# Six block-product groups per column pair, and sums of the features laid out anew, in the last matrix product of a two-block transformer kernel

## The reference, cut to what matters

```python
def conv_ffn(h, w_up, conv_w, conv_b, w_down):
    S = h.shape[1]
    val, gate = jnp.split(h @ w_up, 2, axis=-1)
    gp = jnp.pad(gate, ((0, 0), (CONV_W - 1, 0), (0, 0)))
    g = conv_b
    for i in range(CONV_W):
        g = g + conv_w[i] * gp[:, i:i + S]
    return (jax.nn.silu(g) * val) @ w_down
    ...
        x = x + conv_ffn(rms_norm_2(x, norm_ffn[l]), w_up[l], conv_w[l], conv_b[l], w_down[l])
    return rms_norm_2(x, norm_final)
```

## Time and profile before

| | |
|---|---|
| median of 3 runs | 2433.54 us (2433.43 to 2433.71) |
| the profiled execution: its own time | 2433.6 us |
| its span | 2431.8 us |
| TensorE, busy | 2421.5 us |
| VectorE, busy | 1717.2 us |
| ScalarE, busy | 1381.1 us |
| GpSimd, busy | 83.4 us |

### The profile page before, as it was taken

The page is one execution under the profiler, slowest core; times in us unless marked ns, Lnnn a source line. Parts: engine busy times, 40 slices in busy tenths (PEclk is TensorE's granted clock), DMA queues, the critical chain, the costliest instruction groups (busy, mean ns, idle before and its releaser), DMA issues.

```text
span 2431.8 us, 34028 instructions
## 1 busy us (share of the span) xinstructions
PE 2421.5 (100%) x12669; PEld 2081.3 (86%) x12669; DVE 1717.2 (71%) x2079; ACT 1381.1 (57%) x1830; POOL 83.4 (3%) x101
## 2 busy tenths in 40 slices
PE   9999999999999999999999999999999999999998
PEld 8888888888889999888888888888988888888877
DVE  7675757888765656786656767665666666679997
ACT  6444444556656666565755556565645545556655
POOL 0000000001100000010000000000000000000001
PEclk9999999999999999999999999999999999999999
DMA  8666666676556554575585564455566665657775
GB/s 314 199 189 185 188 188 184 197 243 216 182 175 181 178 160 144 210 230 191 163 237 165 157 176 146 165 180 156 174 188 181 186 193 179 188 173 211 240 233 162
DMA packets 237363, 462.46 MB, mean 190 GB/s; under 512 B 15265, under 2 KB 60753, under 8 KB 236220
## 3 DMA queue, kind: packets, MB, share of 16 engines
q1 hardware_dynamic: 230960, 435.94, 57.5%
q0 software_dynamic: 5888, 24.34, 3.8%
q10 hardware_dynamic: 396, 0.59, 0.2%
HBM read 448.68 MB, written 2.69 MB: 186 GB/s over the span
## 4 chain that ended last, share of the span: by engine, by line
PE 98%; DVE 1%; ACT 0%; DMA 0%; issue 0%; ACTq 0%; SPq 0%; DVEq 0%
PE ps L835 25%; PE ps L837 13%; PE ps L801 12%; PE ps L803 12%; PE ps L802 12%; PE ps L985 6%; PE ps L986 6%; PE ps L987 6%; PE ps L759 1%; PE ps L868 1%; PE ps L866 1%; PE ps L867 1%; PE ps L1473 1%; PE ps L1244 0%; PE ps L1232 0%; PE ps L1431 0%
## 5 line engine op out<-in xcount | busy, mean ns | idle before, releaser
L2468 DVE TENSOR_TENSOR w_lo<-raw,w_hi 128x1024 fp32r<-128x1024 f32 x689 | 842.3, 1228 | 465.5 <-ACT w_hi L1643 444.8
L1643 ACT ACTIVATE w_hi<-raw 128x1024 fp32r<-128x1024 f32 x689 | 727.0, 1060 | 650.6 <-PE ps L837 358.0
L835 PE MATMUL ps<-x_hi_lo,w_hi 128*128 128x512 f32 x2336 | 820.9, 394 | 1.1 <-DVE w_lo L2643 1.1
L837 PE MATMUL ps<-x_hi_lo,w_lo 128*128 128x256 f32 x2336 | 660.7, 283 | 0.0
L835 PEld LDWEIGHTS ps<-x_hi_lo,w_hi 128*128 128x128 f32 x2336 | 438.7, 188 | 102.7 <-issue 1.2
L801 PE MATMUL ps<-w_hi,x_hi_lo 128*128 128x512 f32 (+3 forms) x1184 | 461.9, 390 | 0.0
L803 PE MATMUL ps<-w_hi,x_hi_lo 128*128 128x512 f32 (+3 forms) x1184 | 453.8, 383 | 0.0
L802 PE MATMUL ps<-w_lo,x_hi_lo 128*128 128x512 f32 (+3 forms) x1184 | 452.6, 382 | 0.0
L837 PEld LDWEIGHTS ps<-x_hi_lo,w_lo 128*128 128x128 f32 x2336 | 439.2, 188 | 0.0
L1820 ACT ACTIVATE w_hi<-raw 128x1024 fp32r<-128x1024 f32 x207 | 215.5, 1051 | 159.8 <-PE ps L987 135.5
L2476 DVE TENSOR_TENSOR w_lo<-raw,w_hi 128x1024 fp32r<-128x1024 f32 x207 | 248.8, 1222 | 34.4 <-ACT w_hi L1820 34.0
(11 more groups left out here) (469 smaller groups left out, 2732.3 us busy)
## 6 DMA issues: line engine op xcount, KB each, us to landing
raw<-in_w_up SPq DMA_DIRECT2D x160, 512.0 KB, 3.8
raw<-in_pool_w_in SPq DMA_DIRECT2D x126, 512.0 KB, 4.0
raw<-in_w_in SPq DMA_DIRECT2D x96, 480.0 KB, 3.9
raw<-in_w_down SPq DMA_DIRECT2D x84, 512.0 KB, 5.3
raw<-in_pool_w_out SPq DMA_DIRECT2D x64, 512.0 KB, 5.3
raw<-in_ple_w_gate SPq DMA_DIRECT2D x64, 512.0 KB, 4.3
raw<-in_mla_w_in SPq DMA_DIRECT2D x56, 448.0 KB, 3.6
raw<-in_pool_w_group SPq DMA_DIRECT2D x32, 512.0 KB, 4.3
```

The lines of the kernel that those rows point to most:

```text
L835: pe.matmul(bank, w_hi[:, slot, cols], xs[:, k].rearrange("p s n -> p (s n)"), start=k == 0, stop=False, skip_group_check=True)
L837: last = pe.matmul(bank[:, 0:T], w_lo[:, slot, cols], xs[:, k, 0, :], start=False, stop=k == nkt - 1, skip_group_check=True)
L1643: act.activation(w_hi[:, t.slot(), :], raw[:, slot, :], ACT.Copy).then_inc(S("w_hi"), 1)
L2468: dve.tensor_tensor(w_lo[:, t.slot(), :], raw[:, u % RAW, :], w_hi[:, t.slot(), :].bitcast(F32), ALU.subtract)\
```

## The change

A sixth group (tiles 16 to 19) is added to each pair, and `DOWN` has a new order in which the first group stands behind six plain products in place of ten. The first three of the four feature-sum steps are taken out of the start of the down product and put between the `w_lo` steps of the last up chunks (`y_pair_sum`); two of their results stand in a place of their own (`fearly`), which lies where `ffn_y_hi` of tiles 16 to 27 comes later. The cuts of the sums now come as five steps on either engine, since the third sum's high part is spread over three places. The cuts of tiles 16 to 19 wait until the low parts of the sums are written. The load of chunk 1's final gain goes behind the last group with the other three.

```diff
-DOWN_QUADS = [20, 24, 28, 32, 36]
-DOWN_WHOLE = [tuple(range(k, min(k + 2, FKT))) for k in (*range(0, 20, 2), 40, 42)]
+DOWN_QUADS = [16, 20, 24, 28, 32, 36]
+DOWN_WHOLE = [tuple(range(k, min(k + 2, FKT))) for k in (*range(0, 16, 2), 40, 42)]
...
-DOWN = [D0[:10] + DQ[:1] + D1[:3] + DQ[1:2] + D1[3:6] + DQ[2:3] + D1[6:8] + DQ[3:4] + D1[8:10] + DQ[4:] + D1[10:] + D0[10:],
-        D2[:4] + DQ[:1] + D2[4:6] + DQ[1:2] + D2[6:8] + DQ[2:3] + D2[8:9] + D3[:1] + DQ[3:4] + D3[1:3] + DQ[4:] + D2[9:] + D3[3:]]
-DOWN_Y_STEPS = {6: 3, 7: 4, 9: 5, 12: 6, 13: 7, 17: 8, 19: 9}
-DOWN_Y = [(0, 8), (8, 16), (16, 20), (20, 24), "sums", (24, 28), (28, 32), (32, 36), (36, 40), (40, 43)]
+DOWN = [D0[:6] + DQ[:1] + D0[6:8] + DQ[1:2] + D1[:2] + DQ[2:3] + D1[2:4] + DQ[3:4] + D1[4:6] + DQ[4:5] + D1[6:8] + DQ[5:] + D1[8:] + D0[8:],
+        D2[:4] + DQ[:1] + D2[4:5] + DQ[1:2] + D2[5:7] + DQ[2:3] + D2[7:8] + DQ[3:4] + D2[8:9] + D3[:1] + DQ[4:5] + D3[1:2] + DQ[5:] + D2[9:] + D3[2:]]
+DOWN_Y = [(0, 8), (8, 16), "sums", (16, 20), (20, 24), (24, 28), (28, 32), (32, 36), (36, 40), (40, 43)]
+DOWN_Y_STEPS = {7: 4, 10: 5, 13: 6, 16: 7, 19: 8, 21: 9}
...
             if DOWN_Y[n] == "sums":
+                products(act, "up")
+                act.wait_ge(S("y_pairs"), 13)
+                for m in range(2):
+                    act.activation(fsums_hi[m], fearly[:, m], ACT.Copy)
                 act.wait_ge(S("y_pairs"), 15)
-                for m in range(3):
-                    last = act.activation(fsums_hi[m], fsums[:, m], ACT.Copy)
+                for (q0, q1), part in fsums_hi4.items():
+                    last = act.activation(part, fsums[:, 2, q0:q1], ACT.Copy)
                 last.then_inc(S("fy_hi"), 1)
             else:
                 k = slice(*DOWN_Y[n])
-                act.wait_ge(S("y_pairs"), 2 * n + 2 if n < 3 else 13)
+                act.wait_ge(S("y_pairs"), 2 * n + 2 if n < 2 else 14)
+                if n > 2:
+                    act.wait_ge(S("fy_lo"), 3)
                 act.activation(fyh[:, k, :], fy[:, k, :], ACT.Copy).then_inc(S("fy_hi"), 1)
...
-        y_hi(2)
...
         assert t.n["unit"] == UNITS_END["up"] + 6, t.n
+        y_hi(2)
+        y_hi(3)
...
-            if n == 27:
+            if n == 25:
                 square_out(2)
...
         y_lo(1)
-        lo(3)
-        y_lo(2)
         lo(2)
+        y_pair_sum(0)
+        lo(1)
+        y_pair_sum(1)
+        lo(1)
+        y_pair_sum(2)
+        lo(1)
         gate_sum(3)
...
         products(dve, "up")
-        y_sum(down, 0, "y_pairs", 11)
-        lo(1)
-        y_sum(down, 1, "y_pairs", 11)
-        lo(1)
-        y_sum(down, 2, "y_pairs", 11)
-        lo(1)
-        y_sum(down, 3, "y_pairs", 11)
+        y_pair_sum(3)
+        lo(3)
+        y_lo(2)
+        y_lo(3)
...
-            if n in (27, 28):
-                quads_out(0, n - 27)
+            if n in (24, 25):
+                quads_out(0, n - 24)
...
-        final_gain(1)
         weight_sums(down.weight_sums)
         pool.wait_ge(S("w_used"), RING + down.quads_end[1])
-        pool.wait_ge(S("final_gain_in"), 16)
-        for c in (0, 2, 3):
+        for c in (1, 0, 2, 3):
             final_gain(c)
+        pool.wait_ge(S("final_gain_in"), 16 * NCH)
```

More of the change, by code:

```diff
@@ L310, in build @@
     ident = fixed("identity", [128, 128])
-    gain = fixed("gain_columns", [128, 512])[:, 0:GAIN_COLS]
+    gain = fixed("gain_columns", [128, GAIN_COLS])
+    CAUSAL = pos[0]
     causal = fixed("causal_mask", [128, 256])
@@ L488, in bank, with sum_hi @@
             return ps[:, (4 * (c // 2) if self.both else 0) + 2 * self.set_of(c) + tt, :]
+        def sum_hi(self, m, q):
+            if self.name == "down" and m == 2:
+                return [part[:, q - qs[0]] for qs, part in fsums_hi4.items() if qs[0] <= q < qs[1]][0]
+            return self.sums_hi[m][:, q]
         def quad_banks(self, p):
@@ L498, in build @@
     nq = len(DOWN_QUADS)
-    FSUMS = 32768 - 6 * 1024 * nq
-    fsums, fsums_lo = (arena(name, FSUMS, [128, 3, nq, 2, 128], dt) for name, dt in (("ffn_y_sums", F32), ("ffn_y_sums_lo", F32R)))
-    fsums_hi = [arena(f"ffn_y_sums_hi{n}", FSUMS + (3 + n) * 1024 * nq, [128, nq, 2, 128], F32R) for n in range(3)]
+    fsums, fsums_lo = (arena(name, 0, [128, 3, nq, 2, 128], dt) for name, dt in (("ffn_y_sums", F32), ("ffn_y_sums_lo", F32R)))
+    fsums_hi = [arena(f"ffn_y_sums_hi{n}", (3 + n) * 1024 * nq, [128, nq, 2, 128], F32R) for n in range(2)]
+    fsums_hi4 = {(0, 2): arena("ffn_y_sums_hi2_first", 5 * 1024 * nq, [128, 2, 2, 128], F32R),
+                 (2, 5): arena("ffn_y_sums_hi2_next", 120832, [128, 3, 2, 128], F32R),
+                 (5, 6): at("ffn_y_sums_hi2_last", CAUSAL, [128, 1, 2, 128], F32R)}
+    fearly = arena("ffn_y_sums_early", 76800 + 1024 * DOWN_QUADS[0], [128, 2, nq, 2, 128])
     psums, psums_lo = (arena(name, 81920, [128, 3, 3, 2, 128], dt) for name, dt in (("pool_y_sums", F32), ("pool_y_sums_lo", F32R)))
     psums_hi = [arena(f"pool_y_sums_hi{n}", off, [128, 3, 2, 128], F32R) for n, off in enumerate((91136, 94208, 106496))]
-    dsum = arena("down_sum", 120832, [128, 512])
+    dsum_late = arena("down_sum", 8192, [128, 512])
     pool_out = Paired("pool_out", y32, yh, yl, POOL_Y, psums, psums_hi, psums_lo, POOL_QUADS, POOL_STEPS, POOL_LOADS,
@@ L1052, in part @@
                     elif name == "T1":
-                        block(i, e5, "e5", x.sums_hi[3][:, q], x.sums_lo[:, 3, q])
+                        block(i, e5, "e5", x.sum_hi(3, q), x.sums_lo[:, 3, q])
                     elif name == "T3":
-                        block(i, e7, "e7", x.sums_hi[0][:, q], x.sums_lo[:, 0, q])
+                        block(i, e7, "e7", x.sum_hi(0, q), x.sums_lo[:, 0, q])
                     elif name == "T2":
-                        block(i, e6, "e6", x.sums_hi[1][:, q], x.sums_lo[:, 1, q])
+                        block(i, e6, "e6", x.sum_hi(1, q), x.sums_lo[:, 1, q])
                     else:
@@ L3461, in y_out, with y_pair_sum @@
             dve.sem_inc(S("part_free"), 1)
+        def y_pair_sum(n):
+            s3, s2, s4 = fearly[:, 0], fearly[:, 1], fsums[:, 2]
+            if n == 0:
+                last = dve.tensor_tensor(s3, down.blocks(0, 0), down.blocks(0, 1), ALU.subtract)
+            elif n == 1:
+                dve.wait_ge(S("y_pairs"), 11)
+                last = dve.tensor_tensor(down.blocks(0, 1), down.blocks(1, 1), down.blocks(0, 1), ALU.subtract)
+            elif n == 2:
+                dve.wait_ge(S("y_pairs"), 12)
+                last = dve.tensor_tensor(s2, down.blocks(0, 1), down.blocks(0, 0), ALU.add)
+            else:
+                dve.wait_ge(S("y_pairs"), 14)
+                last = dve.tensor_tensor(s4, down.blocks(1, 0), s2, ALU.subtract)
+            last.then_inc(S("y_pairs"), 1)
+            t.add("pair")
         def y_lo(n):
@@ L3466, in y_lo @@
             if DOWN_Y[n] == "sums":
-                for m in range(3):
-                    last = dve.tensor_tensor(fsums_lo[:, m], fsums[:, m], fsums_hi[m].bitcast(F32), ALU.subtract)
+                for m in range(2):
+                    dve.tensor_tensor(fsums_lo[:, m], fearly[:, m], fsums_hi[m].bitcast(F32), ALU.subtract)
+                for (q0, q1), part in fsums_hi4.items():
+                    last = dve.tensor_tensor(fsums_lo[:, 2, q0:q1], fsums[:, 2, q0:q1], part.bitcast(F32), ALU.subtract)
             else:
```

7 lines of the change are left out of this document (2 added, 5 removed).

## The result

The changed kernel takes **2449.95 us** (median of 4 runs, 2449.39 to 2451.07), the kernel before 2433.53 beside it: ratio 1.0068, 95% interval 1.0050 to 1.0085. That is slower by 16.4 us where the forecast had 5.0; the time lies outside the range of 2436.0 to 2441.6. The profiled execution took 2450.41 us, span 2448.6, against 2433.6 and 2431.8.

The account below looks back on a forecast made before the run. TensorE, busy 2421.5 of 2431.8 us, was taken as the bound. Removed matmuls -2.8, extra cuts +0.2, up-product sums +0.9, first group +5.5 and ending +1.2 gave +5.0 on 2433.6: 2438.6 us, range 2436.0 to 2441.6.

Parts of the forecast that it names:

- Sum: -2.8 + 0.2 + 0.9 + 5.5 + 1.2: Whole kernel: removed matmuls, extra cuts, up-product sums, first group and ending, together +5.0 us.
- the 2.79 us for a product: Down product: TensorE's time for one plain product, read from two slot releases; half the matmuls take 1.395 us.
- the forecast's 0.9: Last up chunks: feature-sum steps ahead of the w_lo delay TensorE by 0.9 us, between 0.4 and 1.3.
- 5.5 for the group: First group of the down product: a stall plus short waits, +5.5 us, between 4.8 and 6.2.
- 0.2 for the end of the pair: End of the first pair, where group banks are read out: extra cuts cost +0.2 us, between 0 and 0.5.
- The stall ahead of B11: Start of the first group: TensorE waits 3.4 us for the chain of sum cuts and B11's w_lo.
- The ending: After the last group: later gain loads delay GpSimd's third multiplication and the last chain's add, +1.2 us, bound 2.
- Without any queue in front of it the third one starts at -7 and the loss is 0.2: Ending: GpSimd's third gain multiplication, if not queued, starts 7 us before TensorE's end, costing 0.2 us.
- The clock rival: First group's stall: the granted clock falls and parts take 2.79 us, some +3 us, 2441.6; chance 0.16.
- VectorE's pace: First group behind the stall: w_lo steps take 9.1 us where TensorE needs 7.0, 2.1 us in three short waits.
- a clock under 1.00 after 2215: Sign of being wrong: the profile shows the granted clock below 1.00 after 2215, around or after the first group.
- The rule on the shared access to SBUF: Ending: GpSimd's longer multiplication time would hold beside a busy VectorE, giving the ending rival's 2440.8 us; chance 0.11.

Follow-up runs that it names:

- e1: Kernel before with gain_columns at 340 columns instead of 512, so every tile behind lies 672 bytes lower, no instruction changed: 2444.70 us, ratio 1.0046.
- e7: Changed kernel with the first group behind eight plain products instead of six, sums cut between the seventh and eighth product's weights: 2450.29 us.
- e8: Changed kernel with the first final_gain load issued earlier, behind the second group of the last pair: 2449.61 us.
- e11: e7 with one more signal after each of ScalarE's first two sums, so VectorE works at the same time: 2446.60 us.
- e2: Kernel before with gain_columns at 352 columns, tiles behind it 640 bytes lower: 2409.52 us, ratio 0.9908.
- e9: Kernel before with gain_columns at 416 columns, features at distance 512 modulo 1024 from w_hi: 2410.08 us, ratio 0.9908.
- e10: Kernel before with w_hi and w_lo 640 bytes higher and gain_columns at 352 columns, features staying in place: 2413.32 us, ratio 0.9919.
- e5: Kernel before with gain_columns at 352 columns and 640 unused bytes ahead of the arena, so features keep their old place: 2433.50 us, ratio 1.000.
- e6: Kernel before with every tile 384 bytes higher, all distances between tiles unchanged: 2433.81 us, ratio 1.000.
- e3: Kernel before with gain_columns at 368 columns, tiles behind it 576 bytes lower: 2440.52 us, ratio 1.0029.

## Why the prediction was wrong, and where it was right

**The step that failed** is the tally itself: "Sum: -2.8 + 0.2 + 0.9 + 5.5 + 1.2" rests on a list of parts in which everything ahead of the up product's last chunks costs what it cost. The line that shrinks `gain_columns` had no term in it, with no bound on either side. It was worth 11.1 us (e1), more than twice the sum. A stage whose instructions are the same was taken to be the same stage. In the two profiles 10.75 of it lie ahead of the down product (2208.32 in e1, 2197.57 before) and only 0.4 in it (227.04 us, 226.67 before), so the 2.79 us for a product was a sound price. The uneven cycle of single matmuls, which the trace of before shows, was a hint that something disturbs them.

**The parts that were costed** came out together at 5.25 us (changed kernel less e1) for a forecast of 5.0. The two kernels have the tiles behind `gain_columns` at the same places and differ in the change itself. By their profiled executions (spans 2448.6 and 2443.0, 5.6 apart):

- *Up product:* its end moves from 2208.32 to 2209.28, 0.96 us, and that this is the forecast's 0.9 is luck. Counted back from the down product's first matmul, the last 48 matmuls of the up product take 8.89 us for 8.48, and the difference stays 0.41 for the last 1350. So the sums cost 0.4, the lowest value that the prediction allowed. The other 0.55 stand further ahead, where both kernels have the same instructions; single executions differ there by as much (changed kernel, e7, e8 and e11, the same up to there, begin the down product between 2208.70 and 2209.40).
- *Down product:* 230.03 us for 227.04 (2208.32 to 2435.36 in e1), 2.99 more. With the 2.8 us of matmuls taken out that is 5.8 of waits; forecast 5.7 (5.5 for the group, 0.2 for the end of the pair).
- *The stall ahead of B11:* 3.39 us; forecast 3.4. ScalarE idle 5.4 ahead of tiles 16 to 19; forecast about 5. Behind the stall 2.1 us more were lost (the sixth part begins 9.07 us after the first, at 2238.54; its 30 matmuls would take 7.0); forecast 2.1. The wait at the end of the pair is 0.4 us, at 2327.37; forecast 0.2.
- *The ending:* 9.29 us from the last matmul to the end for 7.64 in e1, 1.65 more; forecast 1.2, bound 2. The forecast did not count what VectorE lost beside GpSimd, and put the delay on GpSimd's queue. The sentence that hangs on this was wrong in its reason: "Without any queue in front of it the third one starts at -7 and the loss is 0.2". e8 took that queue away, and the third began 5 us before TensorE's end, with no gain.

So the close total is in part luck as well: the up product's term was 0.5 too high and the ending's 0.45 too low.

**The clock rival** was half right. The granted clock did fall to 0.50 behind the stall, as at the end of the kernel before. But its 3 us on top did not come. Ten matmuls from 2229.47 to 2233.42 took 3.95 us where ten at 0.233 take 2.33: 1.6 lost, and then a single wait of 0.5. The forecast's 2.1 for "VectorE's pace" is that same sum: TensorE, at half its clock, was slow while it would have waited for VectorE anyway. e7, in another order, keeps the clock at 1.00 and takes the same time. One of the signs that the prediction named for being wrong, a clock under 1.00 after 2215, thus came true. Of the 5.8 us of waits in the down product e11 removes 3.7 (in e7's order): 2.7 of them are the handing to and fro between the two engines, which is thereby shown; the cause of the other 1.0 is open, and that the 2.2 us which remain are VectorE's ten steps to a group is argued only.

**The rule on the shared access to SBUF.** The Trainium skill (SBUF - State Buffer, "SBUF: two separate sides") says that a GpSimd operation and a VectorE operation with two SBUF inputs exclude each other for a whole instruction. The trace agrees in kind: the two VectorE steps that grew by 1.1 us both have two SBUF inputs, the add that reads `ps` behind them (L3582, 0.68) did not grow, though neither did the `w_lo` that follows it (1.21, at 2430.56). GpSimd needed 8.13 us for four multiplications beside a busy VectorE and 2.54 for two beside an idle one. No run took the multiplications away, so that they are the cause is read from the traces, not shown by an experiment. The prediction used this rule for GpSimd's time alone and left out what it does to VectorE. The trace of before had it: beside the two multiplications at 2396.34, which took 2.56 us, stands

```profile
2397.82 2.16 DVE L2476 TENSOR_TENSOR w_lo<-raw,w_hi 128x1024 fp32r<-128x1024 f32 x1
```

and beside the two at 2403.41, which took 4.74, every step of VectorE has its usual length. There one engine or the other pays; in the changed kernel both do.

**What stays open.** That a distance which is a multiple of 256 bytes gives the fast pitch, and one 128 off it the slower one, is shown by e2, e9 and e10 against before, e5 and e6. That e1 and e3 are slower still by their distance is likely but not shown: there the features also start off a multiple of 128 bytes, and no run moved all tiles by so little. What collides is open too. A matmul takes its stationary operand from one of the tiles and its moving operand from the other, and VectorE and ScalarE have no part in it by the pitch beside them; but no profile shows reads. Remainders of 32, 96, 160 and 192 were not tried for the features, nor `w_lo` apart from `w_hi`.

## What to carry to other kernels

When a change resizes a tile, it moves every tile behind it, and that is a change to every stage that reads them: list it as a part, and compare the pitch of matmuls in an untouched stage (matmuls per 100 us of a fully busy TensorE) before explaining anything else. To price a change that also moves tiles, run the old instructions at the new places; here that turned an unexplained 16.4 us into 11.1 and 5.25. And before reordering work around a stall, look whether the two engines that feed it wait for each other: two signals more were worth 3.7 us, two products more of cover nothing.

## What the runs showed of the hardware

- **Matmul speed goes by the distance between its operands.** With stationary and moving operands (fp32 words in 128 partitions) a multiple of 256 bytes apart, a pair of 512 and 256 columns took 0.347 us and came as evenly as the trace's hundredths can tell; at 128 from such a multiple 0.351, in a fixed cycle of 0.34 to 0.36; at 64 and 32 from it (e3, e1) 0.353, in e1 in a cycle of 0.34 to 0.37. Over this kernel that is 2409.5, 2433.5, 2440.5 and 2444.7 us. Moving all tiles together changed nothing (e6). The Trainium skill (TensorE: Matmul & The Clock Gate, "Step-by-step: what each phase is for") says that TensorE has two independent read ports, so that loading weights takes nothing from the running matmul; read alone, that gives no reason for the distance to matter. Here the measurement decides: 24 us lie in it. Whether it is these two reads that meet, no run shows.
- **GpSimd and VectorE:** two multiplications of 128x512 cost GpSimd 2.54 us beside an idle VectorE, and beside a busy one 2.56 to 4.74; VectorE steps with two SBUF inputs beside them took their usual time or about 1 us more (1.80 for 0.68, 2.16 to 2.33 for 1.22).
- **The clock** fell behind a stall of 3.4 us and was back by 2234, 4.5 us after work resumed at 2229.47 (0.96 to 2230, 0.50 to 2233, 0.83 to 2234).
